# Second expert matrix in one 16 KB run per partition, with the first product's halves taken in pairs of columns

## Chip, cores and metric

One NeuronCore of a Trainium2 chip runs the whole program in one launch. The metric is the device time in microseconds (us) of one execution; the kernel before took 1648.65 us in the median of three runs.

## What is computed

A trunk of two layers works on 512 tokens of 1024 features in float32. Each layer has a mixer (grouped attention and a convolution in layer 0, differential attention in layer 1) and then a mixture of experts. The change touches only the experts:

```python
def expert_block(args):
    xblk, e = args
    return (jax.nn.silu(xblk @ w1[e]) * (xblk @ w3[e])) @ w2[e]
```

There are 32 experts per layer, in 4 groups of 8; each token goes to 2 experts of one group. `w1[e]` and `w3[e]` are 1024 x 512, `w2[e]` is 512 x 1024, each 2 MB. RMS normalisation, routing, the weights of the two experts and the residual sum stand around it.

## The kernel before

**Blocks.** The tokens of each expert are put in blocks of 64 rows (`SLOT`); the router makes tables of the rows of each block, and an expert has at least one block. With these inputs there are 70 blocks in both layers together, 33 in layer 0 and 37 in layer 1. The engines work a loop over blocks (TensorE: over experts, and within one over its blocks), held together by semaphores.

**One block.** GpSimd gathers 64 rows of 4 KB (`gather`, line 1541) two blocks ahead. TensorE transposes them (`row_transposes`, line 773), VectorE scales them into `xT` (line 1439). The first product (line 793) multiplies `xT`, which is the stationary operand, with the expert's `w1` (j = 0) and `w3` (j = 1), which move: per block 2 halves of the 512 hidden columns (c) x 8 feature chunks (k) x 2 matrices (j), 256 columns each. The trace has two records for each float32 matmul, so 64 records per block. The `w1` part lands in partitions 0 to 63 of a bank, the `w3` part in 64 to 127. ScalarE takes the silu of the first (line 1042), VectorE multiplies it with the second (line 1446) and on the way sorts the columns of the half: even ones first, then odd ones. TensorE transposes the two half products into `hT` (lines 779, 780; ScalarE copies them, line 1045), and the second product (line 808) multiplies `hT` with `w2`. ScalarE copies the result (line 1049) and GpSimd scatters it to DRAM (line 1553). The transposes of a block's hidden values and of the next block's rows stand between the two products on TensorE; line 779 comes behind a wait for the gather of the next rows (line 796).

**Which hidden unit is where.** `w2` lies in SBUF as four rows of 1024 per partition. Before, partition p holds in slot 2c + a the row 256c + 2p + a: two runs of 8 KB, one from each half of the matrix. Half c of the first product is columns 256c to 256c + 255, so its even columns are slot 2c and its odd ones slot 2c + 1 of the second product.

**Weights.** A ring of three slots (`RING`) holds the matrices of three experts. SyncE alone issues the weight transfers, in an order written out by hand. Three experts per layer are loaded during the mixer; the other 29 are refills: `refill` (lines 491 to 498) waits until the first product of the slot's last expert is done, issues `w1` and `w3` of the next one (`load_w13`, line 428: one run of 16 KB per partition each), waits for its second product and issues `w2` (`load_w2`, line 433). All of these go to one DMA queue (q1) over 16 DMA engines; gathers and scatters go to the queue of GpSimd (q0) on the same engines. The mixers' own weights (`raw`) come on q1 too, in runs of 2 KB.

Of the kernel before, what the change touches and what calls it, by code (L numbers as in the profile page):

```python
# [13 lines left out]
TT, KD = T // P, D // P  # L14
# [8 lines left out]
FK = FH // P  # L23
HH = FH // 2
SLOT = 64
# [27 lines left out]
def build(nc, x, consts, params, bucket, norm_final, ev_w_in, ev_w_out, od_w_in, od_w_out, w1, w3, w2, out):  # L53
# [9 lines left out]
    with ctx:  # L63
# [55 lines left out]
        xT = mw.take("xT", [P, KD, SLOT])  # L119
# [8 lines left out]
        W13, W2 = [], []  # L128
# [105 lines left out]
        B = [BB[:, i, :] for i in range(8)]  # L234
# [6 lines left out]
        def sem(name):  # L241
            return ctx.enter_context(nc.semaphore(name))
# [49 lines left out]
        s_w2 = [[sem(f"s_w2_{l}_{s}") for s in range(RING)] for l in range(DEPTH)]  # L292
# [121 lines left out]
        def _(sp):  # L414
# [15 lines left out]

            def load_w2(l, s, e):
                src = slice(e, e + 1) if isinstance(e, int) else bass.ds(e, 1)
                sp.dma_start(W2[s][:, :, :].rearrange("p (c a) d -> p c (a d)", c=2),
                             w2[l, src].rearrange("e (c p a) d -> p (e c) (a d)", c=2, a=2)).then_inc(s_w2[l][s], 16)

            for l in range(DEPTH):
                if l == 0:
# [11 lines left out]
                    load_w13(0, 2, 2)  # L449
                    load_group(sp, 5, (1,))  # L450
                    load_w2(0, 2, 2)
                    sp.wait_ge(s_ulo, 8 * NB_L0)
                    load_w13(0, 1, 1, (1,))
                    sp.wait_ge(s_gdone, 4 * NB_L0)
                    load_w2(0, 0, 0)
                else:
                    tot = sp.snap(sp.value_load(blkI[0:1, NE:NE + 1], min_val=NE, max_val=NBLK))
# [10 lines left out]
                    for h in range(2, C_HEADS):  # L468
                        sp.wait_ge(s_mx[1], 8 * (h - 1))
                        load_bias(sp, h)  # L470
                    sp.wait_ge(s_o[1], C_HEADS)
                    load_w2(1, 1, 1)
                    load_w13(1, 1, 1, (1,))
                    load_group(sp, NB_L0 + NB_L1 - 1, (0,))
# [42 lines left out]
        def _(pe):  # L517
# [246 lines left out]
            def experts(l):  # L764
                pe.wait_ge(s_tabs, l + 1)

                def row_transposes(full):


                    if full:  # L770
                        pe.transpose(B[0][:, 0:P], xg2[:, 0:P], ident)
                    for k in range(1 if full else 0, KD):
                        last = pe.transpose(B[0][:, k * SLOT:k * SLOT + SLOT], xg[:, k * P:k * P + P], ident[0:SLOT, 0:SLOT])  # L773
                    return last

                def hidden_transposes(c):

                    bank = B[(2, 5)[c]]
                    pe.transpose(bank[:, 0:P], hh2[:, 2 * c * P:2 * c * P + P], ident)  # L779
                    return pe.transpose(bank[:, SLOT:2 * SLOT], hh[:, (2 * c + 1) * P:(2 * c + 2) * P], ident[0:SLOT, 0:SLOT])  # L780

                def expert(e, s, use):

                    at = (lambda v: slice(v, v + 1)) if isinstance(e, int) else (lambda v: bass.ds(v, 1))
                    b0 = pe.snap(pe.value_load(blkI[0:1, at(e)], min_val=0, max_val=NBLK))
                    b1 = pe.snap(pe.value_load(blkI[0:1, at(e + 1)], min_val=1, max_val=NBLK))
                    with pe.Fori(b0, b1) as b:
                        pe.wait_ge(s_w13[l][s], 32 * use)
                        pe.wait_ge(s_xT[l], b + 2)
                        for c in range(2):  # L790
                            for k in range(KD):
                                for j in range(2):
                                    last = pe.matmul(B[(1, 4)[c]][j * SLOT:j * SLOT + SLOT, 0:HH], xT[:, k, :],  # L793
                                                     W13[s][:, j, k, c * HH:c * HH + HH], start=k == 0, stop=k == KD - 1)
                            last.then_inc(s_g1[l], 1)
                        pe.wait_ge(s_xg[l], 16 * b + 32)
                        pe.wait_ge(s_h[l], 2 * b + 1)
                        hidden_transposes(0).then_inc(s_htr[l], 1)
                        row_transposes(False).then_inc(s_xtr[l], 1)
                        pe.wait_ge(s_h[l], 2 * b + 2)  # L800
                        hidden_transposes(1).then_inc(s_htr[l], 1)
                        pe.wait_ge(s_w2[l][s], 16 * use)
                        pe.wait_ge(s_yev[l], b + 1)
                        for c in range(2):
                            pe.wait_ge(s_hT[l], 2 * b + c + 1)
                            for k in range(2 * c, 2 * c + 2):
                                for j in range(2):
                                    last = pe.matmul(B[3][j * SLOT:j * SLOT + SLOT, :], hT[:, k, :], W2[s][:, k, j * 512:j * 512 + 512],  # L808
                                                     start=k == 0, stop=k == FK - 1)
                        last.then_inc(s_g2[l], 1)  # L810


                pe.wait_ge(s_xg[l], 16)
                row_transposes(True).then_inc(s_xtr[l], 1)
                with pe.Fori(0, NE // RING) as i:
                    use = pe.snap(i + 1)
                    for s in range(RING):
                        expert(pe.snap(i * RING + s), s, use)
                for e in range(NE // RING * RING, NE):
                    expert(e, e % RING, e // RING + 1)  # L820
# [844 lines left out]
```

## Time and profile before

| | |
|---|---|
| median of three runs | 1648.65 us |
| lowest and highest run | 1646.8 and 1648.89 us |
| profiled execution: its own time, which is its span | 1649.5 us |
| TensorE busy with matmuls | 1426.3 us (86%) |
| VectorE, ScalarE, GpSimd busy | 449.2, 502.9, 217.9 us |
| mean granted clock of TensorE | 0.935 of full speed |
| data moved by DMA | 471.47 MB, 286 GB/s over the span |
| weight transfers of experts (w1, w3, w2) | 192 of 2048 KB, 35.2 us from issue to landing (median) |

The profile is of one execution. Each group of instructions is told by its line, engine and operation, with the shapes and the count; then come its busy time, the mean duration of one, and the engine's idle time before it with what ended it. A share over 1 of the DMA engines comes from packets that overlap. A chain of waits is followed back from the end of the program. The program prints L and a number for a line of the kernel.

### The profile page before, as it was taken

The numbers are of one execution on the slowest core, as the hardware profiler recorded it, in microseconds if no ns is written. First come the engines' busy times: TensorE is split into PE (matmuls) and PEld (weight loads), VectorE is DVE, ScalarE is ACT, GpSimd is POOL, SyncE is SP. The second block draws the span as 40 slices with busy tenths as digits, with TensorE's granted clock in tenths as the row PEclk, the third lists the DMA queues.
The fourth block names the chain that finished last, engine by engine and source line by source line (L and its number), as shares of the span: only waits on it lengthen the run. The fifth ranks groups of instructions, "written<-read, shape, count | busy, mean of one in ns | idle before, by whom it ended". The sixth has DMA issues, their size and how long they took to land.

```text
span 1649.5 us, 26407 instructions
## 1 busy us (share of the span) xinstructions
PE 1426.3 (86%) x10070; PEld 887.6 (54%) x10071; DVE 449.2 (27%) x1033; ACT 502.9 (30%) x967; POOL 217.9 (13%) x344
## 2 busy tenths in 40 slices
PE   7998994997888788787599989978988999889993
PEld 5874684553444444343488735765544555445551
DVE  4435635110101010102433399442111111101114
ACT  4416733222122112211322377431222222212222
POOL 4020000111111111111000000101111121111211
PEclk9999996998999899989699999987999999989997
DMA  4313046899999999997333210576999999999995
GB/s 162 103 66 129 2 179 258 317 404 408 414 409 411 407 413 410 408 412 292 111 117 102 77 45 23 227 278 234 407 417 406 359 378 423 422 414 398 403 400 192
DMA packets 68596, 471.47 MB, mean 286 GB/s; under 512 B 11512, under 2 KB 12664, under 8 KB 35776
## 3 DMA queue, kind: packets, MB, share of 16 engines
q1 hardware_dynamic: 54144, 442.93, 67.5%
q0 software_dynamic: 11520, 17.34, 3.2%
q10 hardware_dynamic: 2880, 10.49, 1.7%
q8 instruction: 36, 0.59, 0.1%
q14 instruction: 16, 0.13, 0.0%
HBM read 465.95 MB, written 25.20 MB: 298 GB/s over the span
## 4 chain that ended last, share of the span: by engine, by line
PE 53%; DMA 37%; DVE 5%; issue 2%; ACT 2%; SPq 0%; POOL 0%; ACTq 0%; DVEq 0%; POOLq 0%
DMA w<-in_w 32%; PE bank L385 18%; PE bank L793 17%; PE bank L808 5%; DMA xg<-hn_dram,icol 4%; PE bank L590 2%; PE bank L686 1%; PE bank L674 1%; PE bank L773 1%; PE bank L650 1%; PE bank L639 1%; DMA YG<-y_dram 1%; PE bank L779 1%; DVE Pm L1297 1%; PE bank L534 1%
## 5 line engine op out<-in xcount | busy, mean ns | idle before, releaser
L793 PE MATMUL bank<-w,xT 128*64 128x256 f32 x4480 | 539.1, 402 | 102.6 <-DMA w<-in_w 100.7
L793 PEld LDWEIGHTS bank<-w,xT 128*64 128x64 f32 x4480 | 341.1, 146 | 323.6 <-issue 186.2
L1446 DVE TENSOR_TENSOR hh<-bank,sgate 64x256 f32<-64x256 f32 x140 | 59.6, 426 | 864.9 <-ACT sgate L1042 864.9
L808 PE MATMUL bank<-w,hT 128*64 128x512 f32 x1120 | 255.8, 598 | 0.0
L1042 ACT ACTIVATE sgate<-bank 64x256 f32<-64x256 f32 x140 | 52.7, 376 | 499.5 <-PE bank L793 499.5
L808 PEld LDWEIGHTS bank<-w,hT 128*64 128x64 f32 x1120 | 74.2, 136 | 124.7 <-issue 119.9
L344 ACT ACTIVATE whi<-raw 128x512 fp32r<-128x512 f32 (+1 forms) x112 | 67.8, 615 | 167.1 <-PE bank L385 151.7
L352 DVE TENSOR_TENSOR wlo<-raw,whi 128x512 fp32r<-128x512 f32 (+1 forms) x112 | 77.5, 702 | 145.2 <-ACT whi L344 145.2
L1049 ACT ACTIVATE ysb<-bank 128x512 f32<-128x512 f32 x70 | 41.8, 597 | 237.8 <-PE bank L808 237.8
L1553 POOL DMA_INDIRECT y_dram<-ysb,rcol x70 | 72.4, 1035 | 195.8 <-ACT ysb L1049 191.6
L385 PE MATMUL bank<-whi,hi 128*128 128x512 f32 x224 | 90.8, 405 | 3.5 <-DVE wlo L352 3.5
L1538 POOL COPY icol<-idxI 64x1 uint32 (+1 forms) x72 | 12.9, 179 | 586.6 <-DVE xT L1439 586.1
L1042 ACT ACT_TABLE_LOAD x70 | 89.8, 1283 | 1.3
L385 PE MATMUL bank<-whi,lo 128*128 128x512 f32 x224 | 88.3, 394 | 0.0
L385 PE MATMUL bank<-wlo,hi 128*128 128x512 f32 x224 | 88.3, 394 | 0.0
L385 PE MATMUL bank<-hi,whi 128*128 128x512 f32 x208 | 82.4, 396 | 2.9 <-DVE lo L1095 2.9
L385 PE MATMUL bank<-hi,wlo 128*128 128x512 f32 x208 | 82.0, 394 | 0.0
L385 PE MATMUL bank<-lo,whi 128*128 128x512 f32 x208 | 81.9, 394 | 0.0
L1541 POOL DMA_INDIRECT xg<-hn_dram,icol x72 | 70.0, 972 | 54.5 <-POOL icol L1538 43.9
L1045 ACT ACTIVATE hT<-bank 128x128 f32<-128x128 f32 x140 | 38.9, 278 | 58.8 <-PE bank L780 53.9
L1439 DVE TENSOR_TENSOR xT<-bank,PR 128x512 f32<-128x512 f32 x72 | 49.8, 692 | 20.6 <-PE bank L773 13.2
L991 ACT ACTIVATE Pm<-Pm,nmx 128x512 f32<-128x512 f32 x64 | 45.7, 714 | 31.5 <-DVE nmx L1301 31.5
(226 smaller groups left out, 1404.9 us busy)
## 6 DMA issues: line engine op xcount, KB each, us to landing
w<-in_w SPq DMA_DIRECT2D x192, 2048.0 KB, 35.2
raw<-in_od_w_in SPq DMA_DIRECT2D x12, 1024.0 KB, 5.2
raw<-in_ev_w_in SPq DMA_DIRECT2D x6, 1024.0 KB, 5.2
raw<-in_ev_w_out SPq DMA_DIRECT2D x4, 1024.0 KB, 8.0
hn_dram<-HN ACTq DMA_DIRECT2D x8, 512.0 KB, 2.8
YG<-y_dram SPq DMA_DIRECT2D x8, 512.0 KB, 6.1
YG<-y_dram ACTq DMA_DIRECT2D x8, 512.0 KB, 6.1
raw<-in_od_w_out SPq DMA_DIRECT2D x4, 1024.0 KB, 9.7
```

The lines of the kernel that those rows point to most:

```text
L344: act.activation(chunked(whi[:, u % 4, 0:w], G, False), chunked(raw[:, c % 2, k % 4, 0:w], G, True), ACT.Copy).then_inc(s_uhi, 1)
L352: dve.tensor_tensor(chunked(wlo[:, u % 4, 0:w], G, False), chunked(raw[:, c % 2, k % 4, 0:w], G, True), chunked(whi[:, u % 4, 0:w].bitcast ...
L385: last = pe.matmul(b, lhsT, rhs, start=(k == 0 and n == 0), stop=(k == KD - 1 and n == 2))
L793: last = pe.matmul(B[(1, 4)[c]][j * SLOT:j * SLOT + SLOT, 0:HH], xT[:, k, :], W13[s][:, j, k, c * HH:c * HH + HH], start=k == 0, stop=k == ...
L808: last = pe.matmul(B[3][j * SLOT:j * SLOT + SLOT, :], hT[:, k, :], W2[s][:, k, j * 512:j * 512 + 512], start=k == 0, stop=k == FK - 1)
L991: act.activation(Pm[:, n % 2, m, :], Pm[:, n % 2, m, :], ACT.Exp, bias=nmx[:, 2 * n % 64 + m:2 * n % 64 + m + 1], accum_out=ssum[:, 2 * n ...
L1042: act.activation(sgate[SLOT:P, c * HH:c * HH + HH], B[(1, 4)[c]][0:SLOT, 0:HH], ACT.Silu).then_inc(s_sg[l], 1)
L1049: act.activation(ysb[:, :], B[3][:, :], ACT.Copy).then_inc(s_yev[l], 1)
L1439: dve.tensor_tensor(xT[:, :, :], B[0][:, :].rearrange("p (k s) -> p k s", k=KD), gain, ALU.mult).then_inc(s_xT[l], 1)
L1446: dve.tensor_tensor(hh[:, c * HH:c * HH + HH].rearrange("q (a p) -> q a p", a=2), B[(1, 4)[c]][SLOT:P, 0:HH].rearrange("q (p a) -> q a p", ...
L1541: pool.indirect_dma_start(out=xg2[0:SLOT, :], out_offset=None, in_=hn_dram[l], in_offset=bass.IndirectOffsetOnAxis(ap=icol[:, :], axis=0), ...
L1553: pool.indirect_dma_start(out=y_dram[l], out_offset=bass.IndirectOffsetOnAxis(ap=rcol[:, :], axis=0), in_=ysb[:, :], in_offset=None, bound ...
```

## The change

`load_w2` reads row 4p + a into slot a of partition p, which is one run of 16 KB per partition. Half c of the first product takes, of every four adjacent columns, the two from 2c on, and writes them to the same 256 columns of the bank, in order. So the columns of half c are the hidden units 4p + 2c + a, which line 1446 sorts by a as before; what follows is unchanged.

```diff
             def load_w2(l, s, e):
                 src = slice(e, e + 1) if isinstance(e, int) else bass.ds(e, 1)
-                sp.dma_start(W2[s][:, :, :].rearrange("p (c a) d -> p c (a d)", c=2),
-                             w2[l, src].rearrange("e (c p a) d -> p (e c) (a d)", c=2, a=2)).then_inc(s_w2[l][s], 16)
+                sp.dma_start(W2[s][:, :, :].rearrange("p a d -> p (a d)"),
+                             w2[l, src].rearrange("e (p a) d -> p (e a d)", a=FK)).then_inc(s_w2[l][s], 16)
...
                         for c in range(2):
                             for k in range(KD):
                                 for j in range(2):
-                                    last = pe.matmul(B[(1, 4)[c]][j * SLOT:j * SLOT + SLOT, 0:HH], xT[:, k, :],
-                                                     W13[s][:, j, k, c * HH:c * HH + HH], start=k == 0, stop=k == KD - 1)
+                                    last = pe.matmul(B[(1, 4)[c]][j * SLOT:j * SLOT + SLOT, 0:HH].rearrange("q (p a) -> q p a", a=2), xT[:, k, :],
+                                                     W13[s][:, j, k, :].rearrange("q (p a) -> q p a", a=FK)[:, :, 2 * c:2 * c + 2],
+                                                     start=k == 0, stop=k == KD - 1)
                             last.then_inc(s_g1[l], 1)
```

## Rows read from the trace of the kernel before

**Rows 1.** The page: busy tenths in 40 slices of the span.
```profile
PE   7998994997888788787599989978988999889993
...
DMA  4313046899999999997333210576999999999995
```

**Rows 2.** Stretches: length, busy PE, PEld, DVE, ACT, POOL; clock, DMA share, GB/s.
```profile
344.00:765.00 421.00, 346.55 (x2419) 188.22 (x2417) 41.11 (x80) 85.34 (x160) 64.26 (x108) 0.92 1.01 408
1125.00:1183.00 58.00, 57.12 (x434) 32.26 (x433) 7.29 (x14) 13.14 (x26) 10.66 (x18) 0.96 0.82 319
1183.00:1262.00 79.00, 68.78 (x488) 37.08 (x488) 8.84 (x17) 18.75 (x35) 13.77 (x24) 0.96 1.01 415
1262.00:1320.00 58.00, 56.75 (x433) 32.44 (x433) 6.60 (x13) 13.15 (x26) 9.96 (x17) 0.97 0.95 370
1320.00:1368.00 48.00, 47.77 (x369) 26.73 (x368) 6.18 (x12) 12.73 (x24) 9.49 (x16) 1.00 0.98 387
1368.00:1492.00 124.00, 107.94 (x770) 58.45 (x770) 13.47 (x26) 27.38 (x53) 20.34 (x35) 0.94 1.01 420
1492.00:1625.00 133.00, 131.49 (x1012) 73.51 (x1008) 17.18 (x34) 34.73 (x66) 24.93 (x42) 1.00 0.95 373
```

**Rows 3.** TensorE's waits (total us, times, longest): 286 to 770, then 1125 to 1625 us.
```profile
PE bank L793 <- DMA w<-in_w: 74.3, 23, 5.6
...
PE bank L793 <- DMA w<-in_w: 26.4, 11, 4.1
PE bank L779 <- DMA xg<-hn_dram,icol: 2.1, 5, 0.6
```

**Rows 4.** Chain of waits, single links of both layers: start us, length, what.
```profile
723.70 41.23 DMA w<-in_w
...
1183.57 31.43 DMA w<-in_w
...
1273.75 9.53 DMA xg<-hn_dram,icol
```

**Rows 5.** DMA queue (packets, MB, engine share): 215 to 223, then 138 to 144 us.
```profile
q1 hardware_dynamic: 222, 3.38, 100.1%
...
q1 hardware_dynamic: 173, 2.57, 100.1%
```

**Rows 6.** The same queue: 228 to 231, then 1047 to 1050 us.
```profile
q1 hardware_dynamic: 154, 1.26, 100.9%
...
q1 hardware_dynamic: 157, 1.29, 101.6%
```

**Rows 7.** The same queue, 868 to 870 us, in the mixer of layer 1.
```profile
q1 hardware_dynamic: 389, 0.78, 99.8%
```

**Rows 8.** DMA queues, 344 to 765 us.
```profile
q1 hardware_dynamic: 14680, 164.48, 95.5%
q0 software_dynamic: 4319, 7.08, 5.0%
```

**Rows 9.** Groups of VectorE by form: lines 1446 and 352.
```profile
L1446 DVE TENSOR_TENSOR hh<-bank,sgate 64x256 f32<-64x256 f32 x140 | 59.6, 426 | 864.9 <-ACT sgate L1042 864.9
...
L352 DVE TENSOR_TENSOR wlo<-raw,whi 128x256 fp32r<-128x256 f32 x8 | 3.3, 425 | 12.2 <-ACT whi L344 12.2
```

**Rows 10.** Groups of ScalarE by form: lines 1025 and 836.
```profile
L1025 ACT ACTIVATE HN<-X,stats 128x1024 f32<-128x1024 f32 x8 | 17.1, 2135 | 11.1 <-PE bank L534 8.7 <-ACT HN L1025 2.5
...
L836 ACT ACTIVATE HN<-X 128x1024 f32<-128x1024 f32 x12 | 12.7, 1057 | 16.1 <-DVE X L1464 12.0 <-DMA X<-in_x 3.1
```

**Rows 11.** Line 793: its group on the page, then one block in the chain.
```profile
L793 PE MATMUL bank<-w,xT 128*64 128x256 f32 x4480 | 539.1, 402 | 102.6 <-DMA w<-in_w 100.7
...
1301.07 6.91 PE bank L793 x64
```

**Rows 12.** Line 1541, the gather: issue to landing in us, least, median, greatest.
```profile
DMA to landing us min/median/max: 2.9/8.5/9.2
```

**Rows 13.** The page: the weights' queue, packets, MB, share of 16 engines.
```profile
q1 hardware_dynamic: 54144, 442.93, 67.5%
```

## Prediction

> **What bounds the kernel now.** I read the slices of the page first: from about 300 to 765 us and from about 1135 to 1610 us the DMA row stands at 9 while TensorE is between 7 and 9 [rows 1]. These are the two expert stages, and the change lies in them alone. The table by stretches separates them [rows 2]. From 344 to 765 us (layer 0) the 16 DMA engines are full, share 1.01 at 408 GB/s, and TensorE works 347 of 421 us: transfers set the pace. Layer 1 alternates: in 1183 to 1262 and 1368 to 1492 us the DMA engines are full and TensorE has gaps; in 1125 to 1183, 1262 to 1368 and 1492 to 1625 us TensorE is busy 98 to 100%, and it sets the pace. The waits of TensorE say the same [rows 3]: line 793 waits for weights for 74.3 us in layer 0 (23 times) and 26.4 us in layer 1 (11 times), and for the row gather only 2.1 us. The chain of waits runs through weight transfers of 31 to 41 us [rows 4], far more than 2 MB need: each is the time in a full queue, so what counts is the engines' rate, not a transfer's latency.
>
> **What 8 KB and 16 KB packets cost.** The change turns 256 packets of 8 KB per second matrix into 128 of 16 KB, the form that the first matrices have. Both forms can be priced alone. In 215 to 223 us only first matrices flow, 3.38 MB at a share of 100.1%: 8 us x 16 engines x 1.001 = 128.1 us of engine time, 0.621 us for each 16 KB; in 138 to 144 us 2.57 MB take 96.1 us, 0.613 us [rows 5]. In 228 to 231 us only a second matrix flows (1.26 MB in 154 packets, 8 KB each): 48 us x 1.009 / 154 = 0.3145 us; in 1047 to 1050 us 48 x 1.016 / 157 = 0.3106 us [rows 6]. The means are 0.617 us for 16 KB and 0.625 us for two times 8 KB: **8 ns saved per packet removed**, with the pairings of these rows giving 0 to 16 ns. A third size agrees: the mixer's weights in runs of 2 KB, 0.78 MB in 32 x 0.998 us [rows 7], cost 0.671 us per 16 KB, so 54 ns for 7 packets more, 8 ns each.
>
> Under the mixed load the price may be higher. From 344 to 765 us the weights' queue held 95.5% of 421 x 16 us, 6433 us of engine time, for 164.48 MB [rows 8]. At the prices above, a third of the bytes in 8 KB packets, it would be 6693 x 0.617 + 6693 x 0.3126 = 6222 us. The excess of 211 us over 13,386 packets is 16 ns each; if all of it goes by the packet, a packet removed saves 24 ns. Part of it must stay, since the gathers and scatters on the other queue (5.0% there) push in between weight packets of any size. So the bounds are 0 and 24 ns; I take 12, nearer to the packets measured alone: 8 plus a quarter of the excess. The Trainium skill, "DMA: Bandwidth & Descriptors", section "Why small descriptors are slow (HBM only)", states a fixed cost of about 3 cycles per packet beside one beat per 32 bytes, hence 3 of 518 beats of such a pair, an estimate of 3.6 ns; the sum below would then be 1.4 us, and the 2 KB row, with 8 ns, is against it.
>
> **The sum.** Per expert 128 packets fewer x 12 ns / 16 engines = 96 ns (0 to 192). It counts where DMA is the pace. In layer 0 all 29 refilled experts pass through the full queue. In layer 1 the queue has been full since the refills began at about 1135 us up to 1262 us, then TensorE is the pace until the queue, idle for a moment near 1317 us (share 0.95 in 1262 to 1320), is full again, and it decides up to 1492 us. With 6.29 MB per expert the stretches carry 58 x 319 GB/s and 79 x 415 GB/s, 8 experts, and 48 x 387 and 124 x 420 GB/s, 11 experts [rows 2]. So 48 x 0.096 = **4.6 us** (0 to 9.2). After 1492 us TensorE works through to the end, and weights landing earlier bring nothing more. The three second matrices preloaded in each layer land beside the mixer; without that cover they would add 6 x 0.096 = 0.6 us.
>
> **The matmuls of line 793.** Their number, columns and output columns stay; what is added is that the moving operand reads two floats, skips two, and so takes half of each 16 bytes over a range twice as long. No matmul of the trace reads so. The nearest row is VectorE: line 1446 takes every second float of both inputs, 256 per partition, in 426 ns; line 352 with 256 adjacent floats of both inputs takes 425 ns [rows 9]. Half of the bytes used, and no price. The far row is ScalarE: line 1025, which takes one float in every 32 bytes, takes 2135 ns against 1057 ns for 1024 adjacent ones (line 836) [rows 10]: a doubling, with one float in eight used. The change is at the density of the first, so I take 0, with a doubling of line 793 as the far end and no gain, since nothing gets shorter. The rest has one answer, nothing: bank layout, line 1446's reading, the second product's addresses and the semaphores are unchanged, SyncE issues the same 64 transfers with the same waits, and nothing is put before another instruction on any queue. What is late next where a wait shrinks is again the next weights; TensorE has 74 us of gaps in layer 0.
>
> The profiled execution spans 1649.5 us, 0.85 us above the median of the three runs (1646.8 to 1648.89, median 1648.65). Against its own span the sum gives 1644.9 us; against the median **1644.0 us**.
>
> **Rivals.** (a) *Only bytes count*: the excess stays and packet cost is at the lower bound, so no engine time is freed. For it: the pairing at 0 ns [rows 5, 6]. Against: the 2 KB row. Time 1648.7 us, chance 0.18. That the transfer would be cut into 8 KB again belongs here; the first matrices, of the same form, do travel in 16 KB packets [rows 5].
>
> (b) *The matmul reads slower*, the case on the other side. Its place is line 793, 70 blocks of 6.91 us when nothing is waited for [rows 11]. At the far end each block grows by 6.91 us: 484 us less the 100.7 us of waits that would vanish, so 2032 us. It decides early: the stretches of layer 1 where TensorE is the pace are 58 + 58 + 48 + 133 = 297 us, 25 blocks of some 12 us, and 4.6 us / 25 = 0.18 us, 2.7% of line 793, uses up the gain; 10% would give 17 us more, 1661 us. In layer 0 the gaps hide up to 74.3 / 33 = 2.2 us a block. For it: TensorE takes 64 x 256 columns in 6.91 us, 0.42 ns each, while line 1446 needs 1.7 ns per element, so the VectorE row does not prove that SBUF can follow here. Against: that row itself. The Trainium skill, "SBUF — State Buffer", section "Door 1: The DMA port swizzle", says that accesses staying in a 16-byte line run at full rate, with at least two hits per line needed; pairs of floats are exactly at that limit, and the VectorE row agrees with it. Chance 0.14.
>
> (c) *Longer packets delay the gather.* A block's rows come on another queue of the same engines, 64 rows of 4 KB, four per engine. If each waits for one weight packet, a third of these now last 0.31 us longer: 4 x 0.31 / 3 = 0.41 us per gather. It lands after 8.5 us in the median and 9.2 us at most [rows 12], and in blocks paced by TensorE it is just in time: the chain already passes through a gather of 9.53 us there [rows 4], and line 779 waited five times, at most 0.6 us [rows 3]. In 25 blocks it would be 10 us: 1648.65 - 4.6 + 10.3 = 1654 us. Against: two thirds of the bytes are in 16 KB packets already, and only 5 blocks waited. The Trainium skill, "DMA: Bandwidth & Descriptors", section "Queues, rings and completion order", has each engine alternate between queues only at the end of a packet, which would make this so; the small waits for the gather so far do not bear it out much. Chance 0.08.
>
> **How the numbers follow.** About 0.2%, 3.3 us, is what a measurement of this kernel can tell from no change. The forecast has chance 0.60, and as its gain runs from 0 to 9.2 us around 4.6, I put 0.43 of it above 3.3 us and 0.17 below. Same is 0.17 + 0.18 (a) + 0.03 of (c) = 0.38; slower is 0.14 (b) + 0.05 of (c) = 0.19; faster 0.43. The range runs from 1648.65 - 9.2 = 1639.5 to 1651 us, which is no gain, the spread of the runs and the mild part of (c); it leaves out (b) and the rest of (c), some 0.19.
>
> **What would show it.** Right: 8192 packets fewer on queue q1 (54,144 before) [rows 13] at the same bytes; line 793 still at 402 ns mean and 6.91 us per unhindered block; a rate in layer 0's full stretch of about 410 to 411 instead of 408 GB/s; its waits for weights still the largest of TensorE's, the stage some 3 us shorter. Line 793 over 7.1 us per unhindered block would show (b); more and longer waits of line 779 for the gather in the TensorE-paced stretches, (c); an unchanged rate with fewer packets, (a). The forecast is wrong if line 793 changes by more than 2.7%, or if the engine time per second matrix does not fall.

## The result, and the profile after

The changed kernel took 1659.26 us in the median of four runs (1654.17 to 1661.56), the kernel before, run beside it, 1648.77 us (1646.8 to 1652.87). The ratio is 1.0047, with a 95% interval of 1.0031 to 1.0064: **slower by about 0.5%**, outside the range given, and on the other side of the forecast. The ratios leave out slow executions, of which there is one, 3599.75 us among the twelve of e9_all_8kb below.

The packets did become longer. The page of the changed kernel has 8192 fewer on the weights' queue than before, with the same bytes ([rows 13]):

```profile
q1 hardware_dynamic: 45952, 442.93, 67.2%
```

Line 793 changed too. Its group on the page of the changed kernel, against [rows 11]: busy 555.7 us where 539.1 us was, a mean of 407 ns where 402 ns was, and less waiting for weights, 88.7 us for 100.7 us.

```profile
L793 PE MATMUL bank<-w,xT 128*64 128x256 f32 x4480 | 555.7, 407 | 90.3 <-DMA w<-in_w 88.7
```

A mean mixes both levels of TensorE's clock. The least and the median of all records (ns, in the view of this one line) say more. First the kernel before, then the changed one:

```profile
L793 PE MATMUL bank<-w,xT x4480: 379/379/689, 286.6 to 1618.8; 128*64 128x256 f32 x195
```

```profile
L793 PE MATMUL bank<-w,xT x4480: 385/388/690, 285.3 to 1621.8; 128*64 128x256 f32 x195
```

The usual record became longer, not the odd one. Whole blocks show by how much. The timeline (start and length in us) has three blocks of layer 1 in each kernel: the first, one where TensorE waits for nothing, and the last; first the kernel before, then the changed one. The first block is the longer one because the granted clock stood at 0.50 when it began (1126 to 1130 us before, 1123 to 1127 us in the changed kernel) and rose to 1.00 within it.

```profile
1125.79 9.20 PE L793 MATMUL bank<-w,xT 128*64 128x256 f32 x64 [0.78 <-DVE xT L1439]
...
1288.31 7.08 PE L793 MATMUL bank<-w,xT 128*64 128x256 f32 x64
...
1612.10 7.08 PE L793 MATMUL bank<-w,xT 128*64 128x256 f32 x64
```

```profile
1122.67 9.91 PE L793 MATMUL bank<-w,xT 128*64 128x256 f32 x64 [0.78 <-DVE xT L1440]
...
1286.03 7.42 PE L793 MATMUL bank<-w,xT 128*64 128x256 f32 x64
...
1614.77 7.42 PE L793 MATMUL bank<-w,xT 128*64 128x256 f32 x64
```

An unhindered block of line 793 takes 7.42 us in place of 7.08 us (the chain's 6.91 us in [rows 11] is the same block counted without its overlap with the work before it; the chain of the changed kernel has 7.25 us): 0.34 us or 4.8% more. From the first block's start to the last one's, layer 1 took 486.3 us before and 492.1 us after; layer 0, measured so, took 478.4 and 477.7 us. The loss is in layer 1.

The waits of TensorE answer to [rows 3]; the stretches are 280 to 775 us (first line), then 1100 to 1640 us:

```profile
PE bank L793 <- DMA w<-in_w: 66.4, 23, 5.4
...
PE bank L793 <- DMA w<-in_w: 22.3, 9, 3.3
...
PE bank L779 <- DMA xg<-hn_dram,icol: 2.2, 4, 1.1
```

In layer 0 the waits for weights went from 74.3 to 66.4 us, again 23 of them: slower matmuls ate gaps that were there anyway. In layer 1 there was less to eat: 22.3 us of waits for weights, 26.4 us before. The waits for the gather stayed, 2.2 us for 2.1 us.

The two stretches of [rows 2] that differ most in what limits them, in the changed kernel (busy PE, PEld, DVE, ACT, POOL; clock, DMA share, GB/s):

```profile
344.00:765.00 421.00, 354.57 (x2433) 185.93 (x2433) 41.03 (x80) 85.19 (x160) 63.97 (x108) 0.93 1.00 406
...
1492.00:1625.00 133.00, 132.70 (x996) 71.56 (x994) 16.98 (x33) 33.20 (x64) 23.81 (x41) 1.00 0.92 363
```

The transfers of layer 0 were not faster: 406 GB/s for 408. At the end of layer 1, TensorE, busy 132.7 of 133 us, issued 996 records where 1012 were. The granted clock was 1.00 there in both kernels, so a lower clock is not the cause.

Two things told ahead of the result need mending. Layer 0 has 32 blocks and layer 1 has 38 (2048 and 2432 records of line 793), not 33 and 37. And the time of an execution lies some 2 us above its span (1654.17 us for a span of 1652.1 us here), so the profiled execution of the kernel before was not 0.85 but about 3 us above the median.

### The profile page after: what moved, and what is told of

It reads as the page before. It is cut to its first block, busy times and chain, and to the rows that moved or that the text cites. A ratio compares the mean times of both kernels' runs of the same rounds, so it can differ in the third digit from the quotient of the medians.

```text
span 1652.1 us, 26407 instructions
## 1 busy us (share of the span) xinstructions
PE 1437.8 (87%) x10070; PEld 874.3 (53%) x10071; DVE 448.7 (27%) x1033; ACT 503.0 (30%) x967; POOL 217.7 (13%) x344
## 4 chain that ended last, share of the span: by engine, by line
PE 59%; DMA 32%; DVE 4%; issue 2%; ACT 2%; SPq 0%; POOL 0%; ACTq 0%; DVEq 0%; POOLq 0%
DMA w<-in_w 26%; PE bank L793 20%; PE bank L385 18%; PE bank L809 7%; DMA xg<-hn_dram,icol 4%; PE bank L590 2%; PE bank L773 1%; PE bank L674 1%; PE bank L686 1%; PE bank L779 1%; PE bank L650 1%; DMA YG<-y_dram 1%; PE bank L639 1%; PE bank L780 1%; PE bank L534 1%
## 5 line engine op out<-in xcount | busy, mean ns | idle before, releaser
L793 PE MATMUL bank<-w,xT 128*64 128x256 f32 x4480 | 555.7, 407 | 90.3 <-DMA w<-in_w 88.7
L793 PEld LDWEIGHTS bank<-w,xT 128*64 128x64 f32 x4480 | 332.0, 142 | 335.3 <-issue 168.7
L1539 POOL COPY icol<-idxI 64x1 uint32 (+1 forms) x72 | 12.8, 177 | 597.8 <-DVE xT L1440 597.2
```

## Experiments

All ten were timed in five rounds beside the kernel before. The table has what they are read by: the ratio to the kernel before with its 95% interval; an unhindered block of line 793 in layer 0 and layer 1; and each layer's stage from its first to its last block, all from the profiled execution's timeline, in us.

| run | ratio | block, layer 0 / 1 | stage, layer 0 / 1 |
|---|---|---|---|
| before | 1 | 7.08 / 7.08 | 478.4 / 486.3 |
| changed | 1.0047 [1.0031, 1.0064] | 7.42 / 7.42 | 477.7 / 492.1 |
| e1_again | 1.0047 [1.0030, 1.0064] | 7.42 / 7.42 | 478.2 / 495.9 |
| e2_read_only | 1.0044 [1.0029, 1.0058] | 7.42 / 7.42 | 478.7 / 495.6 |
| e3_run_only | 1.0053 [1.0033, 1.0072] | 7.08 / 7.08 | 478.1 / 493.4 |
| e4_step2 | 1.0056 [1.0042, 1.0071] | 7.42 / 7.42 | 478.2 / 496.0 |
| e5_layer0 | 1.0012 [0.9999, 1.0024] | 7.42 / 7.08 | 477.6 / 487.8 |
| e6_run_layer1 | 1.0014 [0.9999, 1.0029] | 7.08 / 7.08 | 477.9 / 486.7 |
| e7_runs_of_4 | 1.0005 [0.9991, 1.0020] | 7.08 / 7.08 | 479.3 / 489.0 |
| e8_step4 | 1.1471 [1.1451, 1.1491] | 7.08 / 14.60 | 478.5 / 721.1 |
| e9_all_8kb | 1.0010 [0.9997, 1.0023] | 7.08 / 7.08 | 480.2 / 486.6 |
| e10_all_4kb | 1.0127 [1.0105, 1.0148] | 7.08 / 7.08 | 489.3 / 495.0 |

A stage is read from one execution. Layer 0 took 477.9 to 479.3 us in the four kernels that leave it as it was (before, e6, e7, e8), and layer 1 took 486.3 to 489.0 us in four whose blocks there have the 7.08 us of before (before, e5, e6, e7). Differences of that size say nothing by themselves. In the series of e5 to e8 the kernel before took 1651.32 us, so the times of e5, e6 and e7 lie 0.5 to 1.6 us above the ranges expected for them; their ratios are what counts.

**The changed kernel again (e1_again).** No edit.

> The changed kernel once more, nothing altered. Theory R (the read: two floats taken and two skipped make line 793 slower at the full clock, 7.42 us per unhindered block against 7.08 before, as the first profile shows): the same 7.42 us, a time of 1655 to 1661 us. Rival P (longer packets: the 16 KB runs delay gathers or weights, and the read is a bystander): also slower, but the extra time would stand in longer waits of line 779 for the gather or of line 793 for the weights.

Median 1659.51 us. The first profile had caught the fastest of its runs; this one, with a span of 1658.8 us, is nearer to the median, and its layer 1 takes 495.9 us, 9.6 us more than before. TensorE's waits there, 1100 to 1640 us:

```profile
PE bank L793 <- DMA w<-in_w: 25.6, 9, 6.0
...
PE bank L779 <- DMA xg<-hn_dram,icol: 1.4, 4, 0.5
```

Neither total is longer than before (26.4 and 2.1 us). With 0.34 us a block, 9.6 us are 28 of the 38 blocks; the first profile, with 5.8 us, gives 17. Theory R holds.

**The read without the long packets (e2_read_only).** Edit to the changed kernel:

```diff
-                sp.dma_start(W2[s][:, :, :].rearrange("p a d -> p (a d)"),
-                             w2[l, src].rearrange("e (p a) d -> p (e a d)", a=FK)).then_inc(s_w2[l][s], 16)
+                for c in range(2):
+                    sp.dma_start(W2[s][:, 2 * c:2 * c + 2, :].rearrange("p a d -> p (a d)"),
+                                 w2[l, src].rearrange("e (p c a) d -> c p (e a d)", c=2, a=2)[c]).then_inc(s_w2[l][s], 16)
...
-                        pe.wait_ge(s_w2[l][s], 16 * use)
+                        pe.wait_ge(s_w2[l][s], 32 * use)
```

> The pairs of columns kept, the second matrix in the new order but loaded by two transfers of 8 KB per partition, so packets as before. Theory R: 7.42 us per block stays, and without the gain of longer packets the time is that of the changed kernel or up to 4 us above it, 1658 to 1664 us. Rival P: packets as before, so the time is back at 1647 to 1651 us.

Median 1657.85 us, ratio 1.0044. With packets of 8 KB as before, the whole loss stays and so do the 7.42 us; an unhindered block in the timeline of this run:

```profile
1299.77 7.42 PE L794 MATMUL bank<-w,xT 128*64 128x256 f32 x64
```

The read alone makes the loss. And going from 16 KB back to 8 KB packets costs nothing that the ratios could tell, so the long packets had brought no gain that they can tell either.

**The long packets without the read (e3_run_only).** Edit to the kernel before:

```diff
-                sp.dma_start(W2[s][:, :, :].rearrange("p (c a) d -> p c (a d)", c=2),
-                             w2[l, src].rearrange("e (c p a) d -> p (e c) (a d)", c=2, a=2)).then_inc(s_w2[l][s], 16)
+                sp.dma_start(W2[s][:, :, :].rearrange("p a d -> p (a d)"),
+                             w2[l, src].rearrange("e (p a) d -> p (e a d)", a=FK)).then_inc(s_w2[l][s], 16)
```

> The 16 KB runs kept, the first product's halves contiguous as before; the second product then multiplies hidden values with rows of the second matrix in another order (the work is the same). Theory R: 7.08 us per block, and the gain of fewer packets alone, 2 to 6 us: 1643 to 1647 us. Rival P: 1655 to 1661 us.

Median 1657.81 us, which looks like rival P, but the run does not decide. The page of this run has 4544 records of line 793 in place of 4480:

```profile
L793 PE MATMUL bank<-w,xT 128*64 128x256 f32 x4544 | 543.9, 401 | 98.8 <-DMA w<-in_w 97.2
```

That is one block more: this kernel leaves out the matching order of the columns, so layer 0 hands on other values, which layer 1 routes otherwise. One block is worth some 12 us there. The total can't be used; the block time, 7.08 us, can, and for its 39 blocks layer 1 took 493.4 / 39 = 12.7 us each, no more than the 486.3 / 38 = 12.8 us before. The next two runs ask the same without touching the routing.

**The change in layer 0 alone (e5_layer0).** Edit to the kernel before: the changed `load_w2` and the changed matmul for `l == 0`, the old ones otherwise.

```diff
+                if l == 0:
+                    sp.dma_start(W2[s][:, :, :].rearrange("p a d -> p (a d)"),
+                                 w2[l, src].rearrange("e (p a) d -> p (e a d)", a=FK)).then_inc(s_w2[l][s], 16)
+                else:
...
+                                    if l == 0:
...
+                                                         W13[s][:, j, k, :].rearrange("q (p a) -> q p a", a=FK)[:, :, 2 * c:2 * c + 2],
...
+                                    else:
...
```

> The whole change in layer 0 alone, layer 1 as before. Theory R (the read costs 0.34 us per block, and it counts where TensorE is the pace, which is layer 1): in layer 0 the transfers are the pace and hide it, the stage keeps its 478 us within 1 us, layer 1 is back at 486 us from its first to its last block; 1647 to 1650 us, the same as before. Rival P (the longer packets cost time by themselves): layer 0 would carry half or more of the loss, 1653 to 1656 us.

Median 1651.46 us beside 1651.32 us, ratio 1.0012 [0.9999, 1.0024]: no difference that can be told. The two blocks below are one of layer 0 (line 798, pairs) and one of layer 1 (line 802, contiguous):

```profile
299.51 7.42 PE L798 MATMUL bank<-w,xT 128*64 128x256 f32 x64
...
1299.62 7.08 PE L802 MATMUL bank<-w,xT 128*64 128x256 f32 x64
```

In layer 0 the slower read is paid in full, 32 x 0.34 = 11 us, and hidden in full, because the transfers are the pace (stage 477.6 us). With layer 1 left alone, the loss is gone.

**The long packets in layer 1 alone (e6_run_layer1).** Edit to the kernel before:

```diff
+                if l == 1:
+                    sp.dma_start(W2[s][:, :, :].rearrange("p a d -> p (a d)"),
+                                 w2[l, src].rearrange("e (p a) d -> p (e a d)", a=FK)).then_inc(s_w2[l][s], 16)
+                else:
...
```

> Only the 16 KB runs, only in layer 1, halves contiguous; the second product of layer 1 multiplies hidden values with rows in another order, but the routing, fixed before it, and so the number of blocks stay. Theory R: 7.08 us per block, layer 1 takes 484 to 487 us from its first to its last block, 1646 to 1650 us. Rival P: longer packets delay gathers where TensorE is the pace, so layer 1 takes 490 us or more, with more than 2.1 us of waits of line 779 for the gather, 1654 us or more.

Ratio 1.0014 [0.9999, 1.0029], layer 1 at 486.7 us where 486.3 us was. TensorE's waits in this run, from 1100 to 1640 us:

```profile
PE bank L797 <- DMA w<-in_w: 23.1, 9, 5.5
...
PE bank L783 <- DMA xg<-hn_dram,icol: 3.9, 7, 1.2
```

The waits for weights fell by 3.3 us and those for the gather (line 783 stands for 779) rose by 1.8 us. Neither step is clear of the spread between executions: in e5 and e7, whose layer 1 has the packets of before, the waits for weights were 26.0 and 29.2 us and those for the gather 2.8 and 1.6 us. So a delay of the gather, rival (c) of the prediction, is not shown here. Theory R holds: long packets alone leave layer 1 and the total where they were.

**Every second column (e4_step2).** Edit to the changed kernel, with the rows of the second product to match:

```diff
-                                    last = pe.matmul(B[(1, 4)[c]][j * SLOT:j * SLOT + SLOT, 0:HH].rearrange("q (p a) -> q p a", a=2), xT[:, k, :],
-                                                     W13[s][:, j, k, :].rearrange("q (p a) -> q p a", a=FK)[:, :, 2 * c:2 * c + 2],
+                                    last = pe.matmul(B[(1, 4)[c]][j * SLOT:j * SLOT + SLOT, 0:HH], xT[:, k, :],
+                                                     W13[s][:, j, k, :].rearrange("q (i a) -> q i a", a=2)[:, :, c],
                                                      start=k == 0, stop=k == KD - 1)
...
+                                row = c + 2 * (k % 2)
...
-                                    last = pe.matmul(B[3][j * SLOT:j * SLOT + SLOT, :], hT[:, k, :], W2[s][:, k, j * 512:j * 512 + 512],
+                                    last = pe.matmul(B[3][j * SLOT:j * SLOT + SLOT, :], hT[:, k, :], W2[s][:, row, j * 512:j * 512 + 512],
```

> 16 KB runs, but the halves are the even and the odd columns: one float taken, one skipped, a pattern with a single step instead of pairs (the second product takes the rows to match). If the price comes with the share of each 16 bytes that is used (a half, as with pairs): 7.42 us per block and 1655 to 1661 us. If it comes with the pattern of two levels, whose inner run has only two floats: 7.08 us per block and 1643 to 1647 us.

Median 1659.32 us, and the block as with pairs:

```profile
1300.47 7.42 PE L793 MATMUL bank<-w,xT 128*64 128x256 f32 x64
```

The pattern of two levels is not the price; a pattern with a single step costs the same when it uses the same half of each 16 bytes.

**Four taken, four skipped (e7_runs_of_4), and one of four (e8_step4).** Edits to line 793 of the kernel before, for `l == 1` alone; first e7, then e8:

```diff
...
+                                        last = pe.matmul(B[(1, 4)[c]][j * SLOT:j * SLOT + SLOT, 0:HH].rearrange("q (p a) -> q p a", a=4), xT[:, k, :],
+                                                         W13[s][:, j, k, :].rearrange("q (p a) -> q p a", a=8)[:, :, 4 * c:4 * c + 4],
...
```

```diff
...
+                                        last = pe.matmul(B[(1, 4)[c]][j * SLOT:j * SLOT + SLOT, 0:HH], xT[:, k, :],
+                                                         W13[s][:, j, k // 2 * 2:k // 2 * 2 + 2, :].rearrange("q k (i a) -> q (k i) a", a=4)[:, :, 2 * (k % 2) + c],
...
```

> Everything as before but the read of line 793 in layer 1: four floats taken, four skipped (16 bytes used whole; the hidden columns come in another order, so layer 1's output is another one, with the same blocks). If the price goes by how many 16-byte pieces a read touches: no price, 7.08 us per block in layer 1, 1648 to 1651 us. If any gap costs, or a pattern of two levels: 7.42 us per block, 1657 to 1661 us.

> As the last, but one float of every four is taken (a single step of 16 bytes over two feature chunks; layer 1's output is another one, with the same blocks). If the price goes by 16-byte pieces touched: above 7.42 us per block in layer 1, 7.8 us (price linear in pieces beyond the contiguous read) or up to 14 us (one piece per column at half the rate), so 1665 us or far more. If any gap costs the same: 7.42 us and 1657 to 1661 us.

One unhindered block of layer 1 in each timeline, first e7, then e8:

```profile
1303.79 7.08 PE L794 MATMUL bank<-w,xT 128*64 128x256 f32 x64
```

```profile
1303.42 14.60 PE L794 MATMUL bank<-w,xT 128*64 128x256 f32 x64
```

A gap costs nothing by itself: four floats taken and four skipped read as fast as adjacent ones. One float of each 16 bytes doubles the block, 14.60 us for 7.08 us (2.06 times), and the kernel takes 1894.63 us. Half the granted clock would look much the same (2 x 7.08 = 14.16 us), but the clock of layer 1 in e8 was 1.00 (columns as in [rows 2]):

```profile
1130.00:1600.00 470.00, 470.00 (x2220) 171.23 (x2220) 37.03 (x72) 76.51 (x144) 56.78 (x96) 1.00 0.73 284
```

The patterns fit one sentence. A record streams 256 columns; per block that is 64 x 256 columns, 0.43 ns each at 7.08 us. Read whole, a 16-byte piece serves four columns, 1.73 ns. With one column per piece, e8 spends 14.60 us / (64 x 256) = 0.89 ns per piece; with two, the change spends 7.42 us / (64 x 128) = 0.91 ns per piece. So the read looks bounded by pieces at about 0.9 ns, and pairs, which need one every 0.86 ns to keep up with the columns, fall just short. That is an estimate from the measured patterns, and an interpretation; what sets the limit was not tried.

**Smaller packets (e9_all_8kb, e10_all_4kb).** To see the price of a packet at a size that can be measured, the kernel before got more of them: e9 splits the first matrices into two transfers each, e10 all three into four (the waits count accordingly). The edit of e10; e9 has the first part with 2 in place of 4:

```diff
-                    sp.dma_start(W13[s][:, j, :, :], w[l, src].rearrange("e (p k) f -> p (e k) f", p=P)
-                                 ).then_inc(s_w13[l][s], 16)
+                    for m in range(4):
+                        part = slice(m * KD // 4, (m + 1) * KD // 4)
+                        sp.dma_start(W13[s][:, j, part, :], w[l, src].rearrange("e (p k) f -> p (e k) f", p=P)[:, part, :]
+                                     ).then_inc(s_w13[l][s], 16)
...
+                for c in range(2):
+                    for a in range(2):
+                        sp.dma_start(W2[s][:, 2 * c + a, :], w2[l, src].rearrange("e (c p a) d -> c a p (e d)", c=2, a=2)[c, a]
+                                     ).then_inc(s_w2[l][s], 16)
```

> The kernel before, with the first two matrices also in packets of 8 KB (two transfers each): 768 weight packets per expert in place of 512. Priced at 12 ns per packet, as the forecast did, an expert would take 256 x 12 / 16 = 0.19 us longer and the 29 refills of layer 0 5.6 us: 483.5 to 484.5 us from the first to the last block of layer 0, where 478.4 us was. At 5 ns, what the engine time of the runs so far gives per packet removed, 2.3 us, 480 to 481.5 us. If the size of a packet has no price there, 478 to 479 us.

> The kernel before, with all three matrices in packets of 4 KB (four transfers each): 1536 weight packets per expert in place of 512. At 12 ns per packet 0.77 us per expert, 22 us more in layer 0: about 500 us from its first to its last block. At 5 ns 0.32 us per expert, 9 us more: about 488 us. Without a price 478 to 480 us.

Layer 0 took 480.2 us with 768 packets per expert and 489.3 us with 1536, against 478.4 us with 512. Per packet that is 1.8 x 16 / (256 x 29) = 3.9 ns and 10.9 x 16 / (1024 x 29) = 5.9 ns, the higher one with four times as many transfers in it. The 1.8 us is little more than the spread of the stage, 1.4 us; the 10.9 us is far above it. The expectation at 5 ns (480 to 481.5 us, about 488 us) was met, that at 12 ns was far off.

No run beats both kernels. The candidate that the runs point to, the change where transfers are the pace (e5), is level with the kernel before.

## Why the prediction was wrong

**What bounds the kernel: right.** Layer 0 is paced by transfers and hid 11 us of slower matmuls (e5); layer 1 is largely paced by TensorE and did not. The count of such blocks, 25, lies within the 17 to 29 that the changed kernel, e1, e2 and e4 give at 0.34 us each.

**The matmuls of line 793: the step that failed.** The prediction took 0, from the VectorE row in which line 1446, with half of each 16 bytes used, is as fast as adjacent floats [rows 9]. The price was 0.34 us a block. The flaw stood in the prediction itself: VectorE takes 1.7 ns per element in that row and TensorE 0.43 ns per column, so VectorE needs a 16-byte piece of an input only every 3.3 ns, and its row could not show a limit near 0.9 ns. Besides, one of that row's two inputs is a bank, and only the other, `sgate`, lies where the weights do. The ScalarE row [rows 10], the only one in which a gap had a price, was set aside as the far end. A row of an engine that asks for data more slowly gives no upper bound for one that asks faster; the 0 should have stood as the low end, with the price taken above it. The prediction's own sign of being wrong, line 793 changed by more than 2.7%, came at 4.8%.

**Rival (b) had the mechanism, the place and the point of decision.** It said that 0.18 us a block uses up the gain, and that 10% of line 793 would cost 17 us; at the 4.8% measured its 25 blocks give 8.5 us, and e1 shows 9.6 us. It named the argument that decides, 0.42 ns against 1.7 ns, and still gave it a chance of only 0.14. The Trainium skill, "SBUF — State Buffer", section "Door 1: The DMA port swizzle", states full bandwidth from two hits per 16-byte line; here exactly two hits cost 4.8%, and one hit a factor of 2.06. The measurement decides: two hits are not quite enough for this read.

**The price of a packet: mis-sized.** The term was 12 ns per packet and 4.6 us. The full stretch of layer 0 in the changed kernel answers to [rows 8]:

```profile
q1 hardware_dynamic: 11265, 163.93, 94.9%
```

Engine time per 16 KB of weights went from 421 x 16 x 0.955 / 164.48 MB, 640.8 ns, to 421 x 16 x 0.949 / 163.93 MB, 638.9 ns. Only a third of the bytes changed form, so a packet removed saved three times the difference, some 6 ns. These shares are rounded; over several profiles the means are 641.8 ns (before, e6, e7, e8) and 639.0 ns (the changed kernel, e1, e3, e4, e5), some 8 ns per packet. That is the price that the prediction read from packets alone; the quarter of the excess that it added was not there.

The stage got less than that. At 8 ns the 29 refills of layer 0 would save 128 x 8 / 16 x 29 = 1.9 us. The stage took 477.6 to 478.2 us in the five profiles with long packets and 477.9 to 479.3 us in the four without: half a microsecond in the mean, inside the spread. In layer 1 the prediction counted 19 experts, 1.8 us, and e6 shows no gain. In e9 and e10 the stage gives 3.9 and 5.9 ns per packet, where engine time reckoned as above gives some 6 and 11. Why only a part of the engine time comes out in the stage is not shown.

The estimate by the Trainium skill, "DMA: Bandwidth & Descriptors", section "Why small descriptors are slow (HBM only)", 3.6 ns per packet, is near the 3.9 ns of e9's stage, and below the 5.9 ns of e10's and every figure by engine time.

**Rival (c): not shown.** The gather's median landing went from 8.5 to 8.7 us (8.6 in e1), its longest from 9.2 to 10.5 us; 0.41 us per gather had been feared. Line 779 waited for it no longer than before in the changed kernel and in e1, and the 3.9 us of e6 are not clear of the spread. **Rival (a)** came nearest to what the packets did to the time, no gain that the ratios can tell (e2, e6) where 4.6 us were expected; but its premise, that no engine time is freed, did not hold.

The sum with measured terms: 25 x 0.34 = 8.5 us in layer 1, nothing from the matmuls of layer 0, and for the packets between nothing and 48 x 128 x 8 / 16 = 3.1 us less. That is 5.4 to 8.5 us, within the 5 to 11 us of the interval.

## What to carry to other kernels

Before a moving operand is read with gaps, count how many 16-byte pieces each instruction needs per unit of time at TensorE's full clock: in this kernel whole pieces were free, half-used ones cost 4.8%, and quarter-used ones doubled the time. Merging DMA packets of 8 KB into 16 KB saved some 8 ns of one DMA engine's time for each packet removed, too little to show in the time, and it could not pay for slower matmuls where TensorE is the pace. And an analogous row of another engine is evidence only if that engine asks for data as fast.

## What the runs showed that was not expected

Line 793 with one float of every 16 bytes takes 2.06 times as long, a little over the 14 us that were named as the most for a block, while four floats of every eight cost nothing. Nearly all of the price comes in the step from two floats of each 16 bytes, at 4.8%, to one.

The gather of 64 rows lands sooner beside smaller packets of weights. The gather's line in the kernel before, in e9 and in e10 (issue to landing in us: least, median, greatest) had medians of 8.5, 7.0 and 6.3 us; here e9, then e10:

```profile
DMA to landing us min/median/max: 2.6/7.0/9.0
```

```profile
DMA to landing us min/median/max: 2.8/6.3/8.6
```

This is the direction that rival (c) supposed. That the other queue gets its turn sooner is one reading of it, not tested apart. With 16 KB packets already in two thirds of the bytes, the last third moved the median by 0.2 us in the changed kernel and 0.1 us in e1.
